# Six experts resident ahead of each pass, gate refills first, and norm statistics by four column groups

## The chip, the cores and the metric

One Trainium2 chip, of which the kernel uses one core. The metric is the device time of one execution in microseconds (us), lower is better. TensorE is PE in the profile (PEld is its weight load), VectorE is DVE, ScalarE is ACT, GpSimd is POOL, and SyncE, which here only issues DMAs, is SP.

## The reference

One inference step of a backbone with two layers over 384 tokens of width 1024: 128 context tokens and 256 latent tokens, all in float32. Layer 0 mixes tokens by attention, layer 1 by window means. Then both layers do the same mixture of experts:

```python
def modulate(x, g, shift, scale):
    return rms_norm(x, g) * (1.0 + scale) + shift
...
        x = x + g1 * m
        h = modulate(x, norm_ffn_g[l], sh2, sc2)
        x = x + g2 * hierarchical_moe(h, moe_w_group[l], moe_w_expert[l], moe_w_gate[l],
                                      moe_w_up[l], moe_w_down[l])
```

`hierarchical_moe` takes for each token the best of 4 groups and in it the best 2 of 8 experts. Each of the 32 experts has a gate and an up matrix of 1024x256 and a down matrix of 256x1024 (`silu(x Wg) * (x Wu)`, times the token's weight, times `Wd`). The shifts, scales and gates of the modulation are one product of the conditioning vector with 1024x6144 weights (`ada_w`) in each layer.

## The kernel before

**Order of the work.** Every engine has its own program, written out by hand; semaphores alone order them. The kernel goes through: loads and products of `ada_w` beside the attention of layer 0 (24 chunks of 2 MB, `ada(i)` on TensorE, L1212); the residual (`x_new`); the norm ahead of the experts (`norm_act`, `norm_dve`, `norm_pe`); the router; the pass over 32 expert tiles of 64 tokens (`experts`, `step`), with an extra tile where an expert has more than 64 tokens; the sum of the results (`total`); the pooling mixer of layer 1; then norm, router, pass and sum again.

**Weights in the pass.** An expert has 2 MB of gate and up weights (`moe_w_in`) and 1 MB of down weights (`moe_w_out`). `ring` holds four experts (`RING`), a fifth lies in `more_gu` (half of `adaw`) and `more_down` (a third of `hT`, and half of `adas`). These five are loaded ahead of the pass. SP then issues the other 27 in one queue (`load_tile`): for expert s it waits until the gate product of the expert that held the place is done, issues the 2 MB (L370), waits for its down product, issues the 1 MB (L374), and only then comes to expert s+1. After the fourth refill of layer 0 it issues `bands` and `poolw`, which the mixer of layer 1 needs. The extra tile's weights (`load_extra`) come last, once the down product of expert 28 is done.

**A step on TensorE.** Gate and up products of expert s (L1523, 32 records), the transposes of the rows of expert s+1 (L1499), the down product of expert s-1 (L1547), the transpose of the hidden values (L1532). In steps 1 to 5 six `keep` jobs stand behind it: four transposes (L1466) that bring the residual x from `xT` back to rows by token, which ScalarE copies into `xtok` (L756). GpSimd gathers the rows of each expert by indirect DMA (L531 the first four, L503 the rest) and scatters the results (L513).

**Norm.** x lies as `xT`, features on the partitions: 8 chunks of 128x384. ScalarE squares chunk k into one of two buffers (L688); TensorE adds it up over partitions with a 128x128 matrix of ones (L1403), so every partition gets the sums of all 384 tokens; ScalarE may square chunk k+2 only after that. Then VectorE scales the sums and adds the epsilon (L948), ScalarE takes the root (L690, in layer 0 with a load of its function table), VectorE the reciprocal of 128x384 (L950), and multiplies `xT` by it chunk by chunk (L951, L954).

**Router.** Logits (L1418), a copy, transposes, then a long row of small VectorE operations that picks the experts; counts (L1442, L1445); the rows of h by token (`rows_by_token`, L1433, copied by ScalarE and stored to DRAM); the numbers over 64 (L1453, L1455); places and one table of indices (L1471), from which the gathers start; a second table (L1478); rows of expert 0 (L1499), their copy (L1073), and the first gate product. In layer 0 `ada(21)` and `ada(22)` stand ahead of the logits, `ada(23)` ahead of `rows_by_token(0)`, and VectorE does six operations (`scales` and two more) of layer 1's modulation between the second table and L1073.

## Time and profile before

| | |
|---|---|
| time, median of 3 runs | 889.2 us (885.93 to 895.58) |
| profiled execution, its own time | 891.41 us |
| profiled execution, span | 889.4 us |
| TensorE busy | 725.8 us (82%) |
| VectorE, ScalarE, GpSimd busy | 355.5, 141.0, 175.1 us |
| moved by DMA | 294.32 MB |
| read from and written to HBM, over the span | 354 GB/s |
| mean granted TensorE clock | 0.937 of full speed |

The span runs from the first to the last instruction of the profiled execution. A granted clock of 1.00 is TensorE's upper level, 0.50 its lower one. A busy TensorE may wait inside of it: ends of matmuls are modelled. DMA share is the mean busy share of the core's 16 DMA engines.

### The profile page before, as it was taken

The page shows a single profiled execution, that of the slowest core. Times are in us where ns is not written, and L with a number is a line of the kernel's source. Part 1 is how long each engine was busy: PE and PEld are TensorE (multiplying, and loading weights), DVE is VectorE, ACT ScalarE, POOL GpSimd, SP SyncE. Part 2 cuts the span into 40 slices and gives each one's busy share as a digit, 9 for nine tenths or more (in the row PEclk, how much of TensorE's full clock was granted, in tenths as well). Part 3 has the DMA queues.
Part 4 walks back from the last instruction along what each step waited for, and adds up shares of the span by engine and source line. Part 5 has one row for each costly group of instructions (what it writes and reads, how often), then busy time and mean ns, then how long its engine had stood idle before and what let it go on. Part 6 is the DMA issues. An engine that isn't in the chain of part 4 may idle for free.

```text
span 889.4 us, 12795 instructions
## 1 busy us (share of the span) xinstructions
PE 725.8 (82%) x4544; PEld 404.3 (45%) x4544; DVE 355.5 (40%) x830; ACT 141.0 (16%) x340; POOL 175.1 (20%) x275
## 2 busy tenths in 40 slices
PE   4899989999968999787778872955999978777870
PEld 3333434468636555444444432624655534444430
DVE  2212457742364444323332334465334433333243
ACT  3111154530250110000000012442110000000000
POOL 0000400000002233333223120002133333322220
PEclk9999999999986999999999996985999999999995
DMA  9999849842793799999999947932699999999925
GB/s 343 428 433 405 216 167 410 304 173 102 324 349 103 305 410 418 422 421 421 421 420 422 389 183 291 425 139 88 242 408 376 422 422 421 421 423 422 417 117 213
DMA packets 39237, 294.32 MB, mean 331 GB/s; under 512 B 10568, under 2 KB 12032, under 8 KB 19232
## 3 DMA queue, kind: packets, MB, share of 16 engines
q1 hardware_dynamic: 26512, 275.51, 75.8%
q0 software_dynamic: 10880, 13.26, 5.0%
q10 hardware_dynamic: 1808, 5.06, 1.4%
q8 instruction: 23, 0.38, 0.2%
q14 instruction: 14, 0.11, 0.0%
HBM read 293.24 MB, written 22.02 MB: 354 GB/s over the span
## 4 chain that ended last, share of the span: by engine, by line
PE 53%; DMA 30%; DVE 7%; issue 6%; SPq 2%; ACT 1%; POOL 0%; POOLq 0%; DVEq 0%
DMA ring<-in_moe_w_in 22%; PE bank L1523 15%; PE bank L1287 7%; PE bank L1547 7%; PE bank L1212 4%; PE bank L1386 3%; DMA ring<-in_ada_w 3%; PE bank L1499 2%; DMA ring<-in_moe_w_out 2%; DMA adaw<-results 2%; PE bank L1394 2%; PE bank L1418 2%; PE bank L1346 1%; PE bank L1327 1%; PE bank L1403 1%
## 5 line engine op out<-in xcount | busy, mean ns | idle before, releaser
L1523 PE MATMUL bank<-ring,qkv 128*64 128x256 f32 x2016 | 241.5, 393 | 63.4 <-issue 39.6
L1523 PEld LDWEIGHTS bank<-ring,qkv 128*64 128x64 f32 x2016 | 157.0, 141 | 130.0 <-issue 66.1
L1073 DVE COPY qkv<-bank 128x512 f32<-128x512 f32 x64 | 44.3, 692 | 220.6 <-PE bank L1499 192.6
L513 POOL DMA_INDIRECT results<-adaw,scur x65 | 67.6, 1040 | 311.6 <-DVE adaw L1096 279.3
L1547 PE MATMUL bank<-ring,qkv 128*64 128x512 f32 x504 | 122.0, 604 | 1.2 <-DVE qkv L1085 0.8
L765 ACT ACTIVATE qkv<-bank 128x128 f32<-128x128 f32 x64 | 17.7, 277 | 452.2 <-PE bank L1523 411.8
L503 POOL DMA_INDIRECT adaw<-rows,gcur x57 | 59.1, 1036 | 44.3 <-POOL gcur L500 35.0
L1287 PE MATMUL bank<-ring,hT 128*128 128x512 f32 x144 | 65.2, 609 | 1.3 <-DVE hT L841 1.3
L1547 PEld LDWEIGHTS bank<-ring,qkv 128*64 128x64 f32 x504 | 31.0, 136 | 47.5 <-issue 45.6
L1085 DVE COPY qkv<-bank 128x128 f32<-128x128 f32 x64 | 18.7, 291 | 76.7 <-PE bank L1532 76.7
L1094 DVE SCALAR_TENSOR_TENSOR adaw<-qkv,wcur 128x512 f32<-128x512 f32 x64 | 48.1, 752 | 2.3
L1096 DVE SCALAR_TENSOR_TENSOR adaw<-bank,wcur,adaw 128x512 f32<-128x512 f32 x64 | 48.1, 751 | 2.3
L1499 PE MATMUL bank<-con,adaw 128*128 128x128 f32 x260 | 43.5, 291 | 2.0 <-DVE adaw L1096 2.0
L1287 PEld LDWEIGHTS bank<-ring,hT 128*128 128x128 f32 x144 | 27.4, 194 | 37.8 <-issue 36.5
L1499 PEld LDWEIGHTS bank<-con,adaw 128*128 128x128 f32 x260 | 28.0, 144 | 26.8 <-issue 26.7
L491 POOL MEMSET adaw<- 128x2048 f32 x2 | 3.6, 1805 | 179.5 <-PE bank L1212 146.3
L1532 PEld LDWEIGHTS bank<-con,qkv 128*128 128x128 f32 x64 | 9.0, 140 | 52.7 <-DVE qkv L1079 51.1
L644 ACT ACTIVATE ring<-bank,ss 128x384 f32<-128x384 f32 (+1 forms) x48 | 24.0, 505 | 36.5 <-DVE ss L899 36.5
L1386 PE MATMUL bank<-hT,ring 128*128 128x256 f32 x128 | 29.1, 380 | 0.0
L1212 PE MATMUL bank<-adaw,condT 128*32 128x512 f32 x240 | 28.9, 598 | 0.0
L1386 PEld LDWEIGHTS bank<-hT,ring 128*128 128x128 f32 x128 | 23.7, 190 | 3.7 <-DVE xT L930 0.8
L1532 PE MATMUL bank<-con,qkv 128*128 128x128 f32 x64 | 21.1, 330 | 2.0 <-DVE qkv L1079 2.0
(227 smaller groups left out, 707.9 us busy)
## 6 DMA issues: line engine op xcount, KB each, us to landing
ring<-in_moe_w_in SPq DMA_DIRECT2D x63, 2048.0 KB
ring<-in_moe_w_out SPq DMA_DIRECT2D x63, 1024.0 KB
adaw<-in_ada_w SPq DMA_DIRECT2D x15, 2048.0 KB, 10.7
ring<-in_ada_w SPq DMA_DIRECT2D x9, 2048.0 KB, 10.6
ring<-in_attn_w_qkv SPq DMA_DIRECT2D x3, 2048.0 KB, 35.5
ring<-in_attn_w_o SPq DMA_DIRECT2D x1, 4096.0 KB, 21.4
adaw<-in_moe_w_in SPq DMA_DIRECT2D x2, 2048.0 KB, 23.9
adaw<-results SPq DMA_DIRECT2D x8, 512.0 KB, 6.1
```

Source lines behind the costliest of these rows:

```text
L503: pool.indirect_dma_start(xg[:, b], None, rows, bass.IndirectOffsetOnAxis(ap=gcur[:, b:b + 1], axis=0), bounds_check=row_limit, oob_is_err ...
L513: pool.indirect_dma_start(res, bass.IndirectOffsetOnAxis(ap=scur[:, p, :], axis=0), yout[:, p], None, bounds_check=res_limit, oob_is_err=F ...
L1073: V.tensor_copy(xgT[:, p], bank[2][:, :]).then_inc(xgT_ready, 1)
L1094: V.scalar_tensor_tensor(yout[:, p], gdiff, wcur[:, p, 1:2], glat, ALU.mult, ALU.add).then_inc(y_order, 1)
L1096: V.scalar_tensor_tensor(yout[:, p], bank[4 + p % 2][:, :], wcur[:, p, 0:1], yout[:, p], ALU.mult, ALU.mult)\
L1212: last = T.matmul(out[32 * j:32 * j + 32, :], condT[:, k, c:c + 32], w[:, k], start=i == SETS[n] and half == 0, stop=i + 1 == SETS[n + 1] ...
L1287: last = T.matmul(bank[5 + g % 3][:, :], hT[:, k, t * P:(t + 1) * P], wqkv[n][:, k, :], start=k == 0, stop=k == KD - 1)
L1386: last = T.matmul(bank[WO_BANKS[d % 2]][:, 0:NTOK - CTX], wo[:, k, d * P:(d + 1) * P], hT[:, k, CTX:NTOK], start=k == 0, stop=k == KD - 1)
L1499: last = T.transpose(bank[2][:, i * P:(i + 1) * P], xg[:, q, i * P:(i + 1) * P], ident)
L1523: last = T.matmul(bank[p][64 * a:64 * a + 64, 0:2 * P], xk[:, k % 4, k // 4], w[:, :, k, a * P:(a + 1) * P], start=k == 0, stop=k == KD - ...
L1532: T.transpose(bank[3][:, 0:P], hid[:, p], ident).then_inc(hid_mm, 1)
L1547: last = T.matmul(bank[4 + p][64 * a:64 * a + 64, :], hidT[:, p, 64 * j:64 * j + 64], w[j][:, a * 512:(a + 1) * 512], start=j == 0, stop=j ...
```

## The change

- **Sixth expert.** A place for expert 5 (`RING + 1`): 1.5 MB of its gate and up weights in `xT`, 0.5 MB in the other half of `adas`, the down weights in two thirds of `hT`. SP issues the first two once all `keep` jobs have read `xT`, the last once the rows of expert 0 are transposed. 26 experts are left to refill. So that `xT` can be split, the gate and up weights are laid out chunk by chunk (gate, up, gate, up) instead of all gate, then all up.
- **Gate refills first.** SP issues the 2 MB of expert s and behind it the 1 MB of expert s-1.
- **`bands` and `poolw`** leave the pass: `bands` is loaded in the router of layer 0, `poolw` behind the results of layer 0. For this the rows by token are written to `qkv` (`rows_out`) and not to `xtok`.
- **`keep` jobs** leave the steps: four stand ahead of the first table (L1471), two ahead of the second (L1478).
- **Norm.** All eight chunks are squared into buffers of their own. TensorE adds them up with 32 columns of ones, chunk k into column group k mod 4. ScalarE copies the sums, three one-column matmuls turn them to tokens on partitions, ScalarE and VectorE make root and reciprocal on 128x3, VectorE multiplies them into three identities (128x384), and one matmul with ones spreads the factors over all partitions. VectorE reads them from PSUM.
- **`ada` chunks.** `ada(21)` and `ada(22)` come behind the transposes of the logits, `ada(23)` behind `rows_by_token(5)`; what waits for them (the load of expert 3 among it) moves along.
- **`scales`** of layer 1 move behind the pass of layer 0.

```diff
-        sq = free[:, 3200:3200 + 2 * NTOK].rearrange("p (b n) -> p b n", b=2)
-        rstd = free[:, 3200 + 2 * NTOK:3200 + 3 * NTOK]
-
+        sq = free[:, 0:KD * NTOK].rearrange("p (k n) -> p k n", k=KD)
+        sums = free[:, 3200:3200 + NTOK]
+
...
+        IN_X = KD * NTOK // (2 * FE)
+        sixth_gu = [xT[:, :, :].rearrange("p k t -> p (k t)"), adas[:, 2:4, :].rearrange("p a n -> p (a n)")]
+        sixth_down = flat_h[:, 0:2 * D]
...
-        s_more, s_more_out = sem("s_more"), sem("s_more_out")
-        LAST = [NE - RING + (b + 1) % RING for b in range(RING)]
-        PER_LAYER = [2 + (LAST[b] - RING - 1 - b) // RING for b in range(RING)]
+        s_more, s_more_out, s_six, s_six_out = map(sem, ("s_more", "s_more_out", "s_six", "s_six_out"))
+        AHEAD = RING + 2
+        LAST = [NE - RING + (b + 2) % RING for b in range(RING)]
+        PER_LAYER = [2 + (LAST[b] - AHEAD - b) // RING for b in range(RING)]
+        EXTRA_SLOT = LAST.index(min(LAST))
...
-
-                def load_tile(s, b, old):
-
+                if l == 0:
+                    sp.wait_ge(s_rowsout, 48)
+                    sp.dma_start(bands, bands_in).then_inc(s_bands, 16)
+                    sp.wait_ge(ada_vec, 4)
+                sp.wait_ge(x1_mm, l * 6 + 6)
+                for part, a, b in ((sixth_gu[0], 0, IN_X), (sixth_gu[1], IN_X, KD)):
+                    sp.dma_start(part, moe_w_in[l, RING + 1, :, a * 2 * FE:b * 2 * FE]).then_inc(s_six, 16)
+                sp.wait_ge(xg_mm, l * NE + 1)
+                sp.dma_start(sixth_down, moe_w_out[l, RING + 1]).then_inc(s_six_out, 16)
+
...
+                def refill_in(s, b, old):
                     sp.wait_ge(gu_mm, s + (l * NE + 1 - old))
                     load_in(l, s, b, s_win[b])
+
+                def refill_out(s, b, old):
                     sp.wait_ge(down_mm, s + (l * NE + 1 - old))
                     load_out(l, s, b, s_wout[b])
...
-                for s in range(RING + 1, 2 * RING + 1):
-                    load_tile(s, s - RING - 1, RING + 1)
-                if l == 0:
-
-                    sp.wait_ge(tab_mm, 2)
-                    sp.dma_start(bands, bands_in).then_inc(s_pool, 16)
-                    sp.dma_start(poolw, pool_w[0].rearrange("g (k p) n -> p g k n", p=P)).then_inc(s_pool, 16)
-                loops = (NE - 2 * RING - 1) // RING
+                def refill(s, b):
+
+                    refill_in(s, b, RING)
+                    refill_out(s - 1, (b - 1) % RING, RING)
+
+                for b in range(RING):
+                    refill_in(AHEAD + b, b, AHEAD)
+                    if b:
+                        refill_out(AHEAD + b - 1, b - 1, AHEAD)
+                refill_in(AHEAD + RING, 0, RING)
+                refill_out(AHEAD + RING - 1, RING - 1, AHEAD)
+                first = AHEAD + RING + 1
...
                     for b in range(RING):
-                        load_tile(r * RING + (2 * RING + 1 + b), b, RING)
-                for s in range(2 * RING + 1 + RING * loops, NE):
-                    load_tile(s, (s - 1) % RING, RING)
+                        refill(r * RING + (first + b), (b + 1) % RING)
+                for s in range(first + RING * loops, NE):
+                    refill(s, (s - 2) % RING)
+                refill_out(NE - 1, (NE - 3) % RING, RING)
...
+                if l == 0:
+                    sp.dma_start(poolw, pool_w[0].rearrange("g (k p) n -> p g k n", p=P)).then_inc(s_pool, 16)
...
-                    if i >= 2:
-                        act.wait_ge(st_mm, m * KD + i - 1)
-                    A.activation(sq[:, i % 2], xT[:, k, :], ACT.Square).then_inc(sq_ready, 1)
-                act.wait_ge(ms_ready, m + 1)
-                A.activation(rstd, rstd, ACT.Sqrt).then_inc(std_ready, 1)
+                    A.activation(sq[:, i], xT[:, k, :], ACT.Square).then_inc(sq_ready, 1)
+                act.wait_ge(st_mm, m * 3 + 1)
+                A.activation(sums, bank[STAT_BANKS[m]][:, 0:NTOK], ACT.Copy).then_inc(std_ready, 1)
+                act.wait_ge(st_mm, m * 3 + 2)
+                A.activation(ss[:, 8:11], bank[STAT_BANKS[m]][:, NTOK:NTOK + TT], ACT.Sqrt, scale=1.0 / (32 * D), bias=C("eps"))\
+                    .then_inc(std_ready, 1)
...
-                    act.wait_ge(s_rowsout, l * 48 + 48)
-                    A.activation(xtok[:, t, q * 512:(q + 1) * 512], bank[6 + n % 2][:, :], ACT.Copy).then_inc(x1_copied, 1)
+                    A.activation(xtok[:, t, q * 512:(q + 1) * 512], bank[4 + n % 2][:, :], ACT.Copy).then_inc(x1_copied, 1)
...
+                for n in range(6):
+                    keep(n)
...
-                    for n in KEEP_AT[s]:
-                        keep(n)
...
-                dve.wait_ge(st_mm, m * KD + KD)
-                V.tensor_scalar(rstd, bank[STAT_BANKS[m]][:, 0:NTOK], 1.0 / D, EPS, ALU.mult, ALU.add).then_inc(ms_ready, 1)
-                dve.wait_ge(std_ready, m + 1)
-                order(V.reciprocal(rstd, rstd))
+                dve.wait_ge(std_ready, m * 2 + 2)
+                order(V.reciprocal(ss[:, 12:15], ss[:, 8:11]))
+                V.tensor_tensor(dg[:, :, :], ident.unsqueeze(1).to_broadcast([P, TT, P]),
+                                ss[:, 12:15].unsqueeze(2).to_broadcast([P, TT, P]), ALU.mult).then_inc(root_ready, 1)
+                rstd = bank[STAT_BANKS[m]][:, 0:NTOK]
+                dve.wait_ge(st_mm, m * 3 + 3)
                 V.tensor_tensor(hT[:, 0, :], xT[:, 0, :], rstd, ALU.mult).then_inc(xr_ready, 1)
...
-                if l == 0:
-                    scales(1, 1, 8)
-                    scales(1, 4, 24)
-                    m = mods[:, 1, 2 * KD:3 * KD, :]
-                    order(V.tensor_tensor(m, m, gains[:, 32:40].unsqueeze(2).to_broadcast([P, KD, 2]), ALU.mult))
-                    order(V.tensor_scalar(constant[:, :, :], mods[:, 1, 0:KD, :], C("column_sum"), None, ALU.mult))
-                    V.memset(ss[:, 18:19], 0.0).then_inc(mods_ready, 1)
...
+            scales(1, 1, 8)
+            scales(1, 4, 24)
+            m = mods[:, 1, 2 * KD:3 * KD, :]
+            order(V.tensor_tensor(m, m, gains[:, 32:40].unsqueeze(2).to_broadcast([P, KD, 2]), ALU.mult))
+            order(V.tensor_scalar(constant[:, :, :], mods[:, 1, 0:KD, :], C("column_sum"), None, ALU.mult))
+            V.memset(ss[:, 18:19], 0.0).then_inc(mods_ready, 1)
             total(0, TILES_BACK[0])
...
                 for k in range(KD):
-                    pe.wait_ge(sq_ready, n // 2 * KD + k + 1)
-                    T.matmul(bank[STAT_BANKS[n // 2]][:, 0:NTOK], ones, sq[:, k % 2], start=k == 0, stop=k == KD - 1).then_inc(st_mm, 1)
+                    pe.wait_ge(sq_ready, m * KD + k + 1)
+                    j = 32 * (k % 4)
+                    last = T.matmul(stat[j:j + 32, 0:NTOK], ones[:, 0:32], sq[:, k], start=k < 4, stop=k >= 4,
+                                    skip_group_check=True)
+                last.then_inc(st_mm, 1)
+                pe.wait_ge(std_ready, m * 2 + 1)
+                for t in range(TT):
+                    last = T.matmul(stat[:, NTOK + t:NTOK + t + 1], sums[:, t * P:(t + 1) * P], ones[:, 0:1],
+                                    start=True, stop=True)
+                last.then_inc(st_mm, 1)
+                pe.wait_ge(root_ready, m + 1)
+                T.matmul(stat[:, 0:NTOK], ones, dg[:, :, :].rearrange("p t n -> p (t n)"),
+                         start=True, stop=True).then_inc(st_mm, 1)
 
...
                 norm_pe(2 * l)
                 if l == 0:
                     pe.wait_ge(x_new[0], KD)
                     vectors(2)
-                    ada(21)
-                    ada(22)
...
                 if l == 0:
-                    ada(23)
+                    ada(21)
+                    ada(22)
...
                 rows_by_token(4)
                 rows_by_token(5)
+                if l == 0:
+                    ada(23)
...
                     if n < 2:
-                        pe.wait_ge(gates_read, l + 1)
+                        pe.wait_ge(hb_copied, l * 6 + 6)
                     else:
                         pe.wait_ge(x1_copied, l * 6 + n - 1)
...
 
+                for n in range(4):
+                    keep(n)
...
+                keep(4)
+                keep(5)
                 pe.wait_ge(slots_ready, l * 12 + 12)
```

## Rows read from the trace of the kernel before

**Rows 1.** Windows: busy us (count) of PE, PEld, DVE, ACT, POOL; clock, DMA share, GB/s.
```profile
354.00:510.00 156.00, 125.08 (x877) 70.72 (x876) 54.60 (x118) 5.27 (x19) 45.68 (x74) 0.99 1.00 417
583.00:619.00 36.00, 22.21 (x95) 14.38 (x95) 21.55 (x85) 13.53 (x19) 4.27 (x4) 0.64 0.25 81
700.00:845.00 145.00, 117.55 (x810) 63.55 (x808) 49.60 (x109) 4.99 (x18) 44.41 (x72) 0.98 1.01 421
```

**Rows 2.** Timeline of SP's queue: start, duration, what; refills of layer 0.
```profile
283.89 0.33 SPq L370 DMA_DIRECT2D ring<-in_moe_w_in  x1
294.19 0.33 SPq L374 DMA_DIRECT2D ring<-in_moe_w_out  x1
...
376.07 0.33 SPq L374 DMA_DIRECT2D ring<-in_moe_w_out  x1
...
497.54 0.33 SPq L374 DMA_DIRECT2D ring<-in_moe_w_out  x1
```

**Rows 3.** Windows of 5 us behind the first refill of either pass.
```profile
289.00:294.00 5.00, 5.00 (x36) 2.82 (x32) 1.58 (x3) 0.28 (x1) 0.00 (x0) 1.00 0.31 134
630.00:635.00 5.00, 5.00 (x38) 3.00 (x34) 1.76 (x4) 0.28 (x1) 0.00 (x0) 1.00 0.36 151
```

**Rows 4.** Timeline of TensorE, layer 0, an expert before its weights are late.
```profile
328.56 3.67 PE L1523 MATMUL bank<-ring,qkv 128*64 128x256 f32 x32
...
334.88 3.67 PE L1523 MATMUL bank<-ring,qkv 128*64 128x256 f32 x32
```

**Rows 5.** Chain that ended last: start, duration, what; extra tile of layer 0.
```profile
508.31 18.27 DMA ring<-in_moe_w_out
```

**Rows 6.** DMA issues: count, KB each, us to landing; two loads of layer 0.
```profile
hT<-in_pool_w SPq DMA_DIRECT2D x1, 1024.0 KB, 15.2
qkv<-in_bands SPq DMA_DIRECT2D x1, 800.0 KB, 12.3
```

**Rows 7.** Timeline of TensorE, last expert of layer 1: gate and up, then down.
```profile
854.19 3.67 PE L1523 MATMUL bank<-ring,qkv 128*64 128x256 f32 x32 [0.90 <-issue]
...
860.22 1.94 PE L1547 MATMUL bank<-ring,qkv 128*64 128x512 f32 x8 [0.38 <-DVE qkv L1085]
```

**Rows 8.** Lines of either norm: duration min/median/max in ns, first and last start.
```profile
L688 ACT ACTIVATE qkv<-xT x16: 522/523/524, 221.1 to 576.9; 128x384 f32<-128x384 f32 x16
L934 DVE SCALAR_TENSOR_TENSOR xT<-bank,mods,xT x8: 350/351/351, 220.7 to 233.2; 128x128 f32<-128x128 f32 x8
L941 DVE SCALAR_TENSOR_TENSOR xT<-bank,mods,xT x16: 350/412/476, 563.4 to 572.6; 128x128 f32<-128x128 f32 x8, 128x256 f32<-128x256 f32 x8
L950 DVE RECIPROCAL qkv<-qkv x2: 2553/2554/2554, 240.4 to 579.6; 128x384 f32<-128x384 f32 x2
L951 DVE TENSOR_TENSOR hT<-xT,qkv x2: 557/558/559, 243.0 to 582.2; 128x384 f32<-128x384 f32 x2
```

**Rows 9.** Timeline of ScalarE, norm of layer 0.
```profile
238.26 1.28 ACT L690 ACT_TABLE_LOAD   x1
```

**Rows 10.** Timeline of TensorE and VectorE, router of layer 0.
```profile
244.41 5.80 PE L1418 MATMUL bank<-hT,wr 128*36 128x384 f32 x16 [0.83 <-DVE hT L956]
251.09 1.92 PE L1212 MATMUL bank<-adaw,condT 128*32 128x512 f32 x16
...
256.75 1.52 PE L1442 MATMUL bank<-rt,con 128*128 128x32 f32 x12 [0.45 <-DVE rt L988]
...
258.49 1.97 PE L1433 MATMUL bank<-con,hT 128*128 128x128 f32 x8
...
272.80 2.79 PE L1478 MATMUL bank<-hT 128*128 128x43 f32 x12 [0.77 <-DVE hT L1040]
...
277.29 0.69 DVE L1073 COPY qkv<-bank 128x512 f32<-128x512 f32 x1
```

**Rows 11.** Timeline of TensorE and GpSimd, router of layer 1.
```profile
583.60 8.30 PE L1418 MATMUL bank<-hT,wr 128*36 128x384 f32 x16 [5.20 <-DVE hT L956]
...
613.81 1.14 POOL L531 DMA_INDIRECT adaw<-rows,gidx  x1 [39.61 <-DVE gidx L1037]
```

More of the change, by code:

```diff
@@ L1571, in _ @@
                 gate_rows()
[L1572 removed]
+                first = AHEAD + 1
+                pe.wait_ge(x1_copied, l * 6 + 6)
                 for s in range(1, first):
                     step(s, s % NBUF, old=s - 1)
[L1575 to L1576 removed]
                 loops = (NE - 1 - first) // RING
```

69 lines of the change are left out of this document (37 added, 32 removed).

## The prediction

> **What bounds the kernel now.** I read the windows first, cut at the stages. In both passes, once the resident experts are used up, the DMA share is 1.00 and 1.01 at 417 and 421 GB/s, while TensorE is busy for only 80% [rows 1]. Then SP's queue: its issues of down weights are 121.47 us apart over 15 experts, 8.10 us each [rows 2]. TensorE alone needs 6.32 us a step, from one gate product to the next [rows 4]. So a pass is a DMA stream: it begins with the first refill and ends with the last one, and TensorE has 1.8 us to spare in every expert. The router of layer 1, the third window, is the opposite: DMA share 0.25, clock 0.64 of full speed, a chain of small steps that hop from engine to engine [rows 1]. What is taken off the stream or off this chain shortens the kernel, microsecond for microsecond; what is moved into the idle queue of the router costs nothing, if it is done before the refills begin.
>
> **The sixth expert.** It takes 3 MB (3.146e6 bytes) off each stream, 7.5 us at 421 GB/s [rows 1], so 15.0 us in both. The pace of 8.10 us contains the rows' own gathers and scatters, which stay; it is the upper bound of the saving, 16.2 us. The 3 MB must be read ahead of the pass instead. In layer 1 DMA engines idle for most of 36 us [rows 1]. In layer 0 the loads between the transposes of the logits and the first refill are expert 3 and the fifth expert (3 MB each), `bands` and the sixth: 9.8 MB, 10.3e6 bytes, or 24 us; from 251 us, where `ada(22)` will now end [rows 10], they are through at 275 if they could be issued back to back. The sixth can't: its gate weights wait for the last `keep`, near 274, and land 5 us later, its down weights near 282. The first refill is due at 283.89 [rows 2]. So they fit, with some 2 us to spare; if the cover fails, the refills start later by what is left over, 2.5 us for the down weights.
>
> **`bands` and `poolw`.** 800 and 1024 KB leave the stream of layer 0 [rows 6]: 1.87e6 bytes, 4.4 us. `bands` goes where the queue of layer 0 is idle, `poolw` behind the results of layer 0, ahead of the loads of layer 1's experts. Those delay nothing, since they wait for a router that is 36 us long; `poolw` itself must land before the pooling products some 20 us later. I cost both at nothing.
>
> **Gate refills first.** After the first refill (2 MB, 5.0 us) SP waits for the down product and the queue runs dry: the next issue comes 10.3 us after the first [rows 2], and the windows behind the first refill show a DMA share of 0.31 and 0.36 [rows 3]. The dry stretch is 10.3 - 5.0 = 5.3 us. In the new order the second gate refill waits only for the gate product of expert 1, which ends 2.6 us before the down product of expert 0 behind it (0.66 + 1.94 us of work on TensorE by the same step). So 2.6 us are won in each layer, 5.2 us; bounds are 0 (another wait ends last) and 5.3 us each. Later in the pass the order changes no rate. At its end it does: the last 3 MB are now 2 MB of gates, then twice 1 MB. Before, the last gate weights land at 854.19 and the down weights 2.5 us later, near 856.7, but the last down product starts only at 860.22 [rows 7], 3.5 us behind its weights, because the whole gate product stands before it. From the landing of the gates to the last down product it is 6.0 us. Now the gates come 5 us before the end, so it starts 1.0 us behind its weights. That gives 2.5 us in layer 1. In layer 0 it gives nothing: there the extra tile follows, its weights are issued at 508.31 and land 18.27 us later [rows 5], right as TensorE asks for them; they stand last in the queue and move with it.
>
> **The norm.** From the last x to the first product with the factors layer 0 takes 243.0 - 233.55 = 9.4 us, layer 1 582.2 - 573.0 = 9.2 us [rows 8]. The new chain: a square 0.52; the last column-group matmul to its reader 1.0 (what the old last matmul took to reach VectorE, I take the same); a copy of 128x384 on ScalarE 0.52; three one-column matmuls 0.45; a root of 128x3 0.2; a reciprocal 0.17 (these three are small and estimated, no row stands for them); the product into `dg` 0.56, as any product of 128x384; the spreading matmul 1.0; six hand-overs of 0.05. That is 4.7 us, against a reciprocal of 2.55 us alone before [rows 8]. In layer 0 the root's function table, 1.28 us [rows 9], now stands between copy and root, with only 0.45 us of matmuls to hide it: 5.5 us. So layer 1 wins 4.4 us, layer 0 3.9 us. No row shows a one-column matmul on `sums` or column groups of 384; from half to twice the chain of 4.7 us, the gain lies between 6.8 and -0.2 us each.
>
> **The router of layer 0 gives it back.** `ada(21)` and `ada(22)` lay under the norm and cost nothing. Now two chunks, 3.84 us, stand where one of 1.92 us stood [rows 10], and the counts behind them had waited only 0.45 us for VectorE: 1.92 - 0.45 = 1.5 us later. `ada(23)` now stands between the last rows and the numbers over 64, on which VectorE waits: 1.9 us at full clock, 3.8 at half. The two `keep` jobs ahead of the second table cost what eight transposes cost in the row of that router at half clock, 1.97 us, less the 0.77 us for which TensorE waited there [rows 10]: 1.2 us. But `scales`, which held the copy of expert 0's rows back for 0.6 us, are gone. Sum: -3.9 + 1.5 + 1.9 + 1.2 - 0.6 = +0.1 us. The other four `keep` jobs lie in 6 us of waiting for VectorE; moved out of the steps they shorten TensorE, which does not bound. `scales` behind the pass lie under the wait for the results.
>
> **The first gather of layer 1** is issued at 613.81 [rows 11], and 2 MB of the sixth expert's gates start about 1 us later. It can be held up by nothing, or by the whole load, 5.0 us. Of its 1.1 us of generation most is over by then, so I take 1.0 us. The Trainium skill, page "DMA: Bandwidth & Descriptors", section "Queues, rings and completion order", says that each DMA engine takes packets from the queue rows in turn. By that rule the gather would not wait for the load's end but alternate with it, near the low end of the range; no row here shows a gather beside such a load alone.
>
> **The sum.** Layer 0: -7.5 - 4.4 - 2.6 + 0.1 = -14.4 us. Layer 1: -7.5 - 2.6 - 2.5 - 4.4 + 1.0 = -16.0 us. Together -30.4: the span of 889.4 becomes 859.0, the profiled execution's own 891.4 becomes 861.0. It was 2.2 us above the median of the three runs, 889.2, so the median to come is 858.8 us.
>
> **Rivals.** (a) The clock falls. The logits of layer 0 took 5.80 us after 0.83 us of waiting, those of layer 1 8.30 us after 5.20 us of waiting [rows 10, 11]: the lower level costs 2.5 us. The new norm takes most of TensorE's work out of its chain, and in layer 0 the two `ada` chunks that filled the gap are gone. If the clock is at its lower level from there on, logits cost 2.5 us more, three `ada` chunks 5.8, eight transposes 1.0: +9.3, so 868 us. The Trainium skill, page "TensorE: Matmul & The Clock Gate", section "Why this matters for your kernels", advises against idle gaps between bursts of matmuls because the clock then drops; by that rule the four column groups speak against the change, and this rival is what it would do. Against it: vectors and the spreading matmul fall into the gap, which is then under 3 us at a time, shorter than the 5.20 us of layer 1. (b) The same, the other way: in layer 1 the gap of 5.20 us is broken up and the clock stays: logits 2.5 us sooner, transposes and tables (2 x 2.8 us at half clock) up to 2.8: 854 us. (c) The change does not do what it says in one part: the sixth loads and the gather get in each other's way, up to 4 us more in layer 1, and late down weights, 2.5 us in each layer: 868 us. (d) TensorE becomes the bound, and the kernel slower than before. In the new layout a gate product reads its 256 columns from two places 1 KB apart instead of 8 KB. If that costs each of the 32 records of a step more than 0.06 us on 3.67/32 = 0.115 us, a step passes 8.1 us and both passes are TensorE's. A pass now takes some 243 us from first gate to last down product (27 x 8.10, 4.4 for the two other loads, 5.3 dry, the rest for its first gate product and its tail). At 0.08 us a record a step is 8.9 us, 32 steps 284 us: twice 41 us lost, 3.5 won outside the passes, 967 us. The point from which it is slower than before is 243 / 32 = 7.6 us a step, 0.04 us a record. Nothing speaks for it: the same engine reads both halves in one pattern today. Without such a price TensorE would come to the last gate product of layer 0 at 328.6 + 24 x 6.32 = 480 us, while the gate weights land near 500 (508.31 + 18.27, less 7.5 for the extra tile, 5.0 for the down weights behind them and the 14.4 us of the sum): it can't bind.
>
> **How the numbers follow.** Forecast 855 to 864, 858.8 likeliest: 0.58. (a) 0.16, (b) 0.10, (c) 0.10, (d) 0.02, and 0.04 for what is between, a stream that saves less than its bytes. The range holds 8 of 10: below it takes in (b) with the pace of 8.1 us (-1.2), 852; above, (a) and (c) at 868 with the upper part of the gap's bound, 870. A measurement of this kernel can tell about 1% from no change. All cases but (d) and part of the rest lie more than 9 us below 889: faster 0.96, same 0.02, slower 0.02.
>
> **What would show it.** Right: DMA share still 1.0 to within some 10 us of each pass's end; SP's down issues still 8.1 us apart; the second refill some 7.7 us after the first instead of 10.3; TensorE's gate product at 6.3 us a step when not late; first product with the factors 5 us behind the last x; the first gate product of layer 0 near 278, of layer 1 some 18 us earlier than now, near 601. Wrong: a pace above 8.1 us, a DMA window below 0.9 in the middle of a pass, clock 0.5 at the logits of layer 0, or rows of expert 0 that wait for their gather.

## The result and the profile after

The changed kernel takes 882.1 us, the median of 4 runs (881.69 to 882.61), against 888.95 us of the kernel before beside it. The ratio is 0.989, with a 95% interval of 0.985 to 0.993. So it is faster by some 7 us, not by the 30 us of the forecast, and outside the range of 852 to 870 us. The profiled execution has a span of 880.3 us, 9.1 us less than the one of before.

I read its trace in the order of the forecast. First the windows, one in the middle of each pass and one over the router of layer 1:

```profile
354.00:500.00 146.00, 125.46 (x877) 66.99 (x871) 54.06 (x116) 5.56 (x20) 48.34 (x78) 0.99 1.01 421
700.00:835.00 135.00, 117.65 (x787) 61.08 (x785) 48.25 (x104) 5.00 (x18) 43.36 (x70) 0.95 1.01 422
581.00:617.00 36.00, 24.45 (x117) 17.97 (x114) 18.79 (x77) 14.55 (x21) 4.54 (x5) 0.69 0.52 186
```

The middle of a pass is the stream that it was [rows 1]: DMA share 1.01, 421 GB/s. In the router's window the share went from 0.25 to 0.52: there the sixth expert's gates are read, and the loads of the other residents, now behind `poolw`, end later than before (a share of 0.65 from 581 to 587, against 0.30 before). The next view is TensorE's timeline where no weights are late:

```profile
325.93 3.67 PE L1572 MATMUL bank<-ring,qkv 128*64 128x256 f32 x32
...
332.25 3.67 PE L1572 MATMUL bank<-ring,qkv 128*64 128x256 f32 x32
```

A step still has 6.32 us and a gate product 3.67 us [rows 4]; the new weight layout costs nothing. The norm's lines follow (duration min/median/max in ns, first and last start in us):

```profile
L712 ACT ACTIVATE qkv<-xT x16: 524/524/526, 220.9 to 572.5; 128x384 f32<-128x384 f32 x16
L714 ACT ACTIVATE qkv<-bank x2: 492/492/492, 234.8 to 574.0; 128x384 f32<-128x384 f32 x2
L716 ACT ACTIVATE ss<-bank,con x2: 264/264/264, 236.6 to 575.4; 128x3 f32<-128x3 f32 x2
L976 DVE RECIPROCAL ss<-ss x2: 176/176/176, 236.9 to 575.7; 128x3 f32<-128x3 f32 x2
L977 DVE TENSOR_TENSOR dg<-con,ss x2: 557/557/557, 237.1 to 575.9; 128x384 f32<-128x384 f32 x2
L981 DVE TENSOR_TENSOR hT<-xT,bank x2: 554/554/555, 239.4 to 577.5; 128x384 f32<-128x384 f32 x2
```

The last x of layer 0 ends at 233.29, so its first product with the factors (L981) comes 6.1 us later; in layer 1 it is 5.0 us. Before it was 9.4 and 9.0 us [rows 8]. The forecast had 5.5 and 4.7 us. The reciprocal of 2.55 us has become one of 0.18 us. Up to here all is as forecast. What is not stands in the chain that ended last (start, duration, what):

```profile
259.92 12.90 DMA rows<-qkv
...
273.77 8.52 DMA adaw<-rows,gidx
...
501.28 22.03 DMA ring<-in_moe_w_out
...
607.79 7.31 DMA adaw<-rows,gidx
```

The first gather of expert rows takes 8.5 us in layer 0 and 7.3 us in layer 1, and the pass waits for both. Rows of expert 0 that wait for their gather were on the forecast's list of what would show it wrong. The first gate product comes at 284.36 in layer 0 (278.03 before; the forecast was near 278) and at 617.18 in layer 1 (619.13 before; the forecast was near 601). Then SP's queue and the windows beside it:

```profile
310.68 0.33 SPq L376 DMA_DIRECT2D ring<-in_moe_w_in  x1
313.13 0.33 SPq L380 DMA_DIRECT2D ring<-in_moe_w_out  x1
329.64 0.33 SPq L376 DMA_DIRECT2D ring<-in_moe_w_in  x1
```

```profile
320.00:325.00 5.00, 5.00 (x42) 2.80 (x40) 2.47 (x6) 0.28 (x1) 1.70 (x3) 1.00 0.81 316
325.00:330.00 5.00, 5.00 (x41) 2.78 (x37) 1.90 (x4) 0.26 (x1) 1.91 (x4) 1.00 0.13 39
330.00:335.00 5.00, 5.00 (x37) 2.53 (x37) 2.79 (x6) 0.02 (x1) 1.35 (x3) 1.00 0.92 332
```

Behind the fourth refill SP issues nothing for 16.5 us, and the DMA engines stand still: 0.13 of their share at 325 to 330. (1.00 - 0.81) x 5 + (1.00 - 0.13) x 5 + (1.00 - 0.92) x 5 = 5.7 us of the stream are lost, a second dry stretch that the forecast did not have. Layer 1 has the same gap, from 646.79 to 663.29, and loses 6.7 us by the same sum (shares of 0.97, 0.43, 0.35 and 0.92 from 650 to 670).

### The profile page after: what moved, and what is told of

It reads as the page before. It is cut to its first block, busy times and chain, and to the rows that moved or that the text cites. A ratio compares the mean times of both kernels' runs of the same rounds, so it can differ in the third digit from the quotient of the medians.

```text
span 880.3 us, 12828 instructions
## 1 busy us (share of the span) xinstructions
PE 731.0 (83%) x4560; PEld 404.0 (46%) x4560; DVE 352.0 (40%) x830; ACT 141.5 (16%) x342; POOL 175.7 (20%) x275
## 3 DMA queue, kind: packets, MB, share of 16 engines
q1 hardware_dynamic: 26800, 275.51, 76.9%
q0 software_dynamic: 10880, 13.26, 4.9%
## 4 chain that ended last, share of the span: by engine, by line
PE 54%; DMA 36%; DVE 4%; issue 2%; ACT 2%; SPq 1%; POOL 0%; POOLq 0%; DVEq 0%; ACTq 0%
DMA ring<-in_moe_w_in 25%; PE bank L1572 17%; PE bank L1316 7%; PE bank L1596 6%; PE bank L1241 4%; PE bank L1415 3%; DMA ring<-in_ada_w 3%; DMA ring<-in_moe_w_out 3%; PE bank L1546 2%; DMA adaw<-rows,gidx 2%; DMA adaw<-results 2%; PE bank L1423 2%; PE bank L1458 2%; PE bank L1375 1%; DMA rows<-qkv 1%
## 5 line engine op out<-in xcount | busy, mean ns | idle before, releaser
L1572 PEld LDWEIGHTS bank<-ring,qkv 128*64 128x64 f32 x1952 | 150.3, 144 | 119.9 <-issue 44.0
L1596 PE MATMUL bank<-ring,qkv 128*64 128x512 f32 x488 | 118.1, 604 | 1.1 <-DVE qkv L1108 0.8
L1596 PEld LDWEIGHTS bank<-ring,qkv 128*64 128x64 f32 x488 | 30.0, 136 | 46.0 <-issue 44.1
L1581 PEld LDWEIGHTS bank<-con,qkv 128*128 128x128 f32 x64 | 9.0, 141 | 52.7 <-DVE qkv L1102 51.1
```

The costliest lines, as they stand in the source:

```text
L1572: last = T.matmul(bank[p][64 * a:64 * a + 64, 0:2 * P], xk[:, k % 4, k // 4], w[k // IN_X if b > RING else 0][:, k % IN_X if b > RING else ...
L1581: T.transpose(bank[3][:, 0:P], hid[:, p], ident).then_inc(hid_mm, 1)
L1596: last = T.matmul(bank[4 + p][64 * a:64 * a + 64, :], hidT[:, p, 64 * j:64 * j + 64], w[j][:, a * 512:(a + 1) * 512], start=j == 0, stop=j ...
```

## The experiments

All ratios are to the kernel before, run beside each kernel; brackets are 95% intervals. The table is worked out from the traces: from the end of the last x to the first gate product (the norm and the router), from there to the gate product of layer 0's extra tile and to the last one of layer 1 (the stream), and from the last x of layer 0 to the end of the span. What lies ahead of that last x is the same code in all kernels, and ends anywhere from 230.0 to 238.2 us; so for the traces the last column is a better measure than the span. There is one trace of each kernel. Where kernels have the same code in a stage, their rows still differ: by 1.3 us in router 0 (44.5, 43.3 and 44.6 for the three with the old norm), and by up to 1.8 us in a stream (227.9 and 226.1). Differences in the table that are smaller than this say nothing by themselves.

| kernel | ratio | router 0 | stream 0 | router 1 | stream 1 | from last x of layer 0 |
|---|---|---|---|---|---|---|
| before | 1 | 44.5 | 248.7 | 46.0 | 235.1 | 655.9 |
| norm alone | 0.996 | 44.6 | 248.4 | 41.5 | 234.5 | 650.6 |
| gate refills first alone | 0.995 | 43.3 | 245.9 | 45.8 | 231.4 | 650.1 |
| bands, poolw alone | 0.996 | 44.6 | 244.6 | 45.7 | 235.7 | 656.0 |
| changed | 0.989 | 51.1 | 239.1 | 44.7 | 227.9 | 647.0 |
| changed, sixth's gates in small loads | 0.979 | 48.7 | 238.0 | 42.4 | 227.4 | 640.0 |
| changed without the sixth | 0.981 | 46.9 | 240.7 | 42.2 | 228.3 | 641.9 |
| the same, keep in the steps | 0.991 | 46.3 | 243.6 | 42.2 | 230.6 | 646.0 |
| sixth's gates later | 0.978 | 45.4 | 239.3 | 41.2 | 226.1 | 636.1 |
| six places once | 0.975 | 51.0 | 233.8 | 45.9 | 219.7 | 634.1 |
| both of these | 0.963 | 46.2 | 234.3 | 41.2 | 219.5 | 624.5 |
| both, ada moved | 0.963 | 43.0 | 234.2 | 40.5 | 219.4 | 622.2 |

**Without the sixth expert.** The loads of the sixth are gone, `AHEAD` is 5.

```diff
-        AHEAD = RING + 2
+        AHEAD = RING + 1
...
-                for part, a, b in ((sixth_gu[0], 0, IN_X), (sixth_gu[1], IN_X, KD)):
-                    sp.dma_start(part, moe_w_in[l, RING + 1, :, a * 2 * FE:b * 2 * FE]).then_inc(s_six, 16)
-                sp.wait_ge(xg_mm, l * NE + 1)
-                sp.dma_start(sixth_down, moe_w_out[l, RING + 1]).then_inc(s_six_out, 16)
```

> The changed kernel without the sixth resident expert: its three loads are gone and experts 5, 6, 7, 8 are the first refills, in gate-first order; the norm and everything else stay. Theory A (two losses eat the sixth: the first gather runs beside the sixth's gate load, which costs about 6 us of layer 0 and 5 us of layer 1, and the queue of refills runs dry a second time for 5.7 us a layer, because a ring of four places has nothing free between refill 9 and the gate product of expert 6): 11 us come back, 2 x (7.5 - 5.7) = 3.6 us are lost, so about 874.5 us, 7.5 us faster than the changed kernel, with the first gate product near 278.5 and no second dry stretch of over 2 us. Theory B (only the gather collides, the sixth is otherwise worth its 7.5 us a layer): 882 - 11 + 15 = 886. Theory C (the sixth is worth all of its 15 us, and the norm or the gate-first order gave less than I summed): 897.

Measured: 876.95 us, ratio 0.981 [0.978, 0.985], against 0.989 [0.985, 0.993] with the sixth. So the sixth expert, costed at a gain of 15 us, gained nothing and more likely made the kernel slower: the two intervals just meet, and from the last x the traces have 647.0 us with it and 641.9 without. Theory C is out, and theory A's 874.5 us is nearer than B's 886. The gather is back at 3.85 us. Theory A had the right parts and too large sizes, though: it gave 11 us back in the routers, and the table has 4.2 and 2.5 us; it took 3.6 us from the streams, and the table has 2.0. And SP's queue shows why the sixth gives the stream so little:

```profile
310.93 0.33 SPq L376 DMA_DIRECT2D ring<-in_moe_w_in  x1
313.38 0.33 SPq L380 DMA_DIRECT2D ring<-in_moe_w_out  x1
323.57 0.33 SPq L376 DMA_DIRECT2D ring<-in_moe_w_in  x1
```

The fifth refill goes into place 0 again, so it waits for the gate product of the first refilled expert: here that is expert 5, and the refill is issued 38.5 us after the first gate product (323.57 - 285.08). With the sixth resident it is expert 6, one TensorE step of 6.32 us later, and it is issued after 45.3 us (329.64 - 284.36). A stream 7.5 us shorter starts its long part 6.8 us later. That leaves 0.7 us, and the streams of the table differ by 1.6 and 0.4 us. With five residents the DMA engines have no such dry stretch: their share is 0.97, 1.02, 1.01 and 0.92 in the four windows of 5 us from 310 to 330, and its lowest in layer 1 is 0.82, from 652 to 657.

**The sixth's gate load after the first gather; six places once; both.** Three kernels. In the first, one wait is moved up:

```diff
+                sp.wait_ge(xg_mm, l * NE + 1)
                 for part, a, b in ((sixth_gu[0], 0, IN_X), (sixth_gu[1], IN_X, KD)):
                     sp.dma_start(part, moe_w_in[l, RING + 1, :, a * 2 * FE:b * 2 * FE]).then_inc(s_six, 16)
-                sp.wait_ge(xg_mm, l * NE + 1)
```

In the second, experts 10 and 11 go into the buffers of the fifth and sixth residents, and the waits and places of experts 12 to 31 follow from that:

```diff
-                for b in range(RING):
-                    refill_in(AHEAD + b, b, AHEAD)
-                    if b:
-                        refill_out(AHEAD + b - 1, b - 1, AHEAD)
+                def again_in(s):
+                    b = s - AHEAD if s < 2 * AHEAD else s % RING
+                    if b < RING:
+                        return refill_in(s, b, AHEAD)
+                    sp.wait_ge(gu_mm, s + (l * NE + 1 - AHEAD))
+                    if b == RING:
+                        sp.dma_start(more_gu, moe_w_in[l, s]).then_inc(s_more, 16)
...
+                for s in range(AHEAD, 4 * RING):
+                    again_in(s)
+                    if s > AHEAD:
+                        again_out(s - 1)
```

> The changed kernel, the sixth expert's gate load held back until the rows of the first expert have been transposed, so that it can't run beside the first gather. Theory A: the first gather of each layer lands 5 to 6 us earlier, the first gate product of layer 0 is near 278.5 instead of 284.4, the second dry stretch stays, 871 us. Rival (the gather is not slow because of that load, but because of the bands or of what the gather is itself): gather stays at 7 to 8.5 us, 882. Rival (the load comes too late for the sixth expert's gate product): a wait of TensorE at the step of expert 5, 878 or more.

> The changed kernel, experts 10 and 11 refilled into the buffers of the fifth and sixth residents as soon as these are free, so that there are six places once over and refill s waits for the gate product of expert s - 6 up to s = 15. The gather's collision stays. Theory A (the second dry stretch is the four-place ring's): no dry stretch near 325 or 659, the stream of weights ends 5.7 us earlier in each layer, 871 us. Rival (the dry stretch is covered, as it was with five residents): 882, with the steps that wait for weights merely beginning elsewhere.

> The two last edits together: the sixth's gate load behind the first gather, and its and the fifth's buffers used again for experts 10 and 11. Theory A: the two losses lie in different places and add up, 860 us, first gate product near 278.5, no second dry stretch. Rival (both feed the same end, the landing of the last refills, and one covers the other): 869 to 871, no better than either alone.

Measured: 873.02 us, ratio 0.978 [0.974, 0.982]; 872.52 us, 0.975 [0.971, 0.979]; 859.53 us, 0.963 [0.959, 0.967]. Theory A gave 871, 871 and 860 us. The chain of the first kernel:

```profile
255.70 12.90 DMA rows<-qkv
...
269.55 3.78 DMA adaw<-rows,gidx
```

The gather takes 3.78 us instead of 8.52 us, though `bands` still runs near it: it was the sixth's load. TensorE does not wait for the late load either: it comes to the sixth expert 6.32 us after the fifth, at 311.22, as at a step without a wait. The row ahead of it, the store of the rows, is as slow as it was; that is another matter, below. The third kernel's queue and window, where the changed kernel stood dry:

```profile
311.35 0.33 SPq L457 DMA_DIRECT2D adaw<-in_moe_w_in  x1
313.81 0.33 SPq L380 DMA_DIRECT2D ring<-in_moe_w_out  x1
317.67 0.33 SPq L460 DMA_DIRECT2D xT<-in_moe_w_in  x1
...
320.13 0.33 SPq L469 DMA_DIRECT2D hT<-in_moe_w_out  x1
```

```profile
320.00:325.00 5.00, 5.00 (x43) 3.01 (x43) 2.31 (x5) 0.28 (x1) 1.36 (x3) 1.00 0.99 412
325.00:330.00 5.00, 5.00 (x41) 2.59 (x37) 2.36 (x6) 0.00 (x0) 1.70 (x3) 1.00 1.02 423
```

The refills of experts 10 and 11 (L457, L460) fill the gap. The two losses lie in different columns of the table and add up. The late load takes 5.7 and 3.5 us off the routers of the changed kernel (45.4 and 41.2 instead of 51.1 and 44.7), and 4.8 and 4.7 us off those of the kernel with six places (46.2 and 41.2 instead of 51.0 and 45.9). The six places take 5.3 and 8.2 us off the streams (233.8 and 219.7 instead of 239.1 and 227.9), and 5.0 and 6.6 us where the load is late. In layer 1 the 8.2 us are 1.5 us more than the dry stretch itself, which is no more than streams of the same code differ by.

**The sixth's gates in eight loads of 2 KB a partition.** In the same place as in the changed kernel:

```diff
-                    sp.dma_start(part, moe_w_in[l, RING + 1, :, a * 2 * FE:b * 2 * FE]).then_inc(s_six, 16)
+                    for c in range(b - a):
+                        sp.dma_start(part[:, c * 2 * FE:(c + 1) * 2 * FE],
+                                     moe_w_in[l, RING + 1, :, (a + c) * 2 * FE:(a + c + 1) * 2 * FE]).then_inc(s_six, 16)
```

> The changed kernel, the sixth expert's gate load cut into eight loads of 2 KB a partition instead of two of 12 and 4 KB, in the same place. The first gather beside it took 8.5 us in layer 0, and 3.8 us without it. Theory E (the engines take one packet of each queue in turn, so a gather waits for one packet of the load at each of its own: with small packets it waits less): gather 5 to 6.5 us, first gate product 2 to 3 us earlier after the gather's issue, about 879 us. Rival (the gather stands behind all bytes issued before it, whatever their packets): 8 to 8.5 us again, 882.

Measured: 874.32 us, ratio 0.979 [0.976, 0.983], and in the chain:

```profile
275.06 6.21 DMA adaw<-rows,gidx
...
605.60 4.46 DMA adaw<-rows,gidx
```

6.2 us instead of 8.5, and 4.5 instead of 7.3. The same bytes beside the gather of layer 0 cost half as much when they come in eight small loads (2.4 us over the 3.8 without that load, instead of 4.7). The time is 5 us under the 879 us expected; the table has 2.4 and 2.3 us in the routers, and the rest is of the size by which its rows scatter. The gather's 5 to 6.5 us were expected if the engines take one packet of each queue in turn. The changed kernel's page has 13.26 MB in 10880 packets on the gathers' queue, 1.2 KB each, and 275.51 MB in 26800 on the weights', 10.3 KB each. Turn about, a gather packet of that size would wait for 10 KB of weights, and the gather would last as long as there are weights.

The Trainium skill, page "DMA: Bandwidth & Descriptors", section "Queues, rings and completion order", says that an engine changes between queue rows only at packet boundaries. The trace fits that rule, but it does not single it out, and no run shows that the page's packet is what the profile counts as one.

The rival, a gather that waits for all bytes issued ahead of it, was expected at 8 to 8.5 us. The 6.2 us do not exclude it, because eight issues also take longer than two. In the changed kernel SP had issued all 2 MB at 274.90, and GpSimd's issue of the gather ended at 274.93. Here SP issues the eight loads from 275.28 on, half a microsecond apart, and GpSimd's issue ends at 276.16, so that two or three of the eight stood ahead of the gather. What is shown is that the sixth's gate load makes the gather late, and that eight small loads halve this; whether by turns or by fewer bytes ahead is not.

**The ada blocks moved.** Added to the kernel with both edits: `ada(21)` and `ada(22)` go into TensorE's two pauses in the norm of layer 0, `ada(23)` behind the overflow products.

```diff
+                if n == 0:
+                    ada(21)
                 pe.wait_ge(std_ready, m * 2 + 1)
...
+                if n == 0:
+                    ada(22)
                 pe.wait_ge(root_ready, m + 1)
...
                 last.then_inc(over_mm, 1)
+                if l == 0:
+                    ada(23)
```

> The last kernel (sixth's gate load late, six places once over) with one more edit: of the three blocks of modulation products, two go from behind the logits into the two pauses of TensorE in layer 0's norm, and the third from ahead of the overflow products to behind them. In that kernel VectorE stands idle 2.93 us for the counts and 3.18 us for the overflow products, and the last rows store takes 12.85 us beside the weights of expert 3 and of the fifth, whose loads wait for these blocks. Theory A (these blocks cost about what I gave them, 1.5 and 1.9 us, and their place also makes the rows store late): the first gather is issued 5 us earlier after the logits' start, the norm gets 1.6 us longer, 856 us. Rival (the gather then waits for something else that is as late, or the longer norm eats it): 859 to 860, no change. Rival (the rows store is slow whatever is loaded beside it): store of 12 to 13 us again, 860.

Measured: 860.36 us, ratio 0.963 [0.960, 0.967], the same as without it; an edit worth 3 us is not resolved by these intervals. By the time alone the second rival (no change) is right. The trace shows part of theory A's mechanism in layer 0 all the same: router 0 is 43.0 instead of 46.2 us, and the first gather is issued 29.0 us after the logits' start instead of 32.9, where 5 us less were expected. The third rival, a store that is slow whatever is loaded beside it, is out. Two rows changed. The logits, in the changed kernel first, with TensorE's two pauses ahead of them, and in this one second:

```profile
235.31 0.83 PE L1440 MATMUL bank<-con,qkv 128*128 128x1 f32 x6 [0.58 <-ACT qkv L714]
237.69 1.65 PE L1444 MATMUL bank<-dg,con 128*128 128x384 f32 x2 [1.55 <-DVE dg L977]
...
240.80 7.08 PE L1458 MATMUL bank<-hT,wr 128*36 128x384 f32 x16
```

```profile
244.06 5.78 PE L1484 MATMUL bank<-hT,wr 128*36 128x384 f32 x16 [0.66 <-DVE hT L1008]
```

and the stores of the rows in the list of DMA issues (count, KB each, median us to landing), again the changed kernel first:

```profile
rows<-qkv ACTq DMA_DIRECT2D x3, 512.0 KB, 12.1
```

```profile
rows<-qkv ACTq DMA_DIRECT2D x3, 512.0 KB, 6.4
```

Before, these stores took 4.8 us. They run beside whatever waits for `ada(22)`, the weights of expert 3 and of the fifth. SP issued these 0.8 us ahead of the logits' start before (243.64 against 244.41), 11.7 us behind it in the changed kernel (252.46 against 240.80), and 2.2 us ahead of it here (241.82 against 244.06). VectorE's waits for the counts and for the overflow products are 2.73 and 2.54 us instead of 2.93 and 3.18 us, so of what I had laid on these blocks' own time little was there. The logits of layer 0 took 6.9 to 8.3 us in all seven kernels that have the new norm with empty pauses and the logits right behind it; this is the only one in which they did not.

**The parts alone.** On the kernel before: the new norm; the gate-first order of refills; `bands` behind the stored rows and `poolw` behind the results. Their edits are those of the diff ahead of the prediction, so the last alone is shown:

```diff
-                    sp.wait_ge(tab_mm, 2)
-                    sp.dma_start(bands, bands_in).then_inc(s_pool, 16)
...
+                if l == 0:
+                    sp.wait_ge(s_rowsout, 48)
+                    sp.dma_start(bands, bands_in).then_inc(s_bands, 16)
```

> The kernel before with the new norm alone (statistics by four column groups, factors on 128 x 3, spread by a product with the diagonal matrix). My sum gave this 3.9 us in layer 0 and 4.4 us in layer 1. Theory A (the norm did what was forecast and the loss was elsewhere): 8 us under the kernel before, ratio 0.991. Rival (the shorter norm is given back, by a lower granted clock in the logits that follow, 7.1 us instead of 5.8 us in the changed kernel, or by waits for loads that don't move with it): 4 us or less, ratio 0.996 or more.

> The kernel before with the gate-first order of refills alone, five residents. My sum gave it 2.6 us in each layer for the first dry stretch and 2.5 us in the tail of layer 1, 7.7 us. Theory A: 7 us under the kernel before, ratio 0.992. Rival (the order only moves the wait: the gate weights come sooner and the down weights of the expert ahead later, so the end of the stream stays where it was): ratio 0.998 to 1.0.

> The kernel before with one edit: bands goes behind the fifth expert's loads, after the rows are stored, and poolw behind the results of layer 0, instead of both behind the first four refills. My sum gave this 4.4 us, for 1.87e6 bytes less in the stream of layer 0: 4 us under the kernel before, ratio 0.995, the whole of it between the first and the last gate product of layer 0. Rival (bands now lies beside the rows' own traffic and makes the first gather late, or poolw is late for the pooling products): ratio 0.998 to 1.002.

Measured: 888.33 us, ratio 0.996 [0.993, 0.998]; 887.48 us, 0.995 [0.993, 0.998]; 889.07 us, 0.996 [0.995, 0.998]. By the table `bands` and `poolw` gave 4.1 us of stream 0, the order 2.8 us of stream 0 and 3.7 us of stream 1. The order's 0.995 lies between its theory (0.992) and its rival (0.998 to 1.0). Of the 4.1 us of `bands` and `poolw` nothing is left in that trace from the last x to the end (656.0 against 655.9 us): the extra tile's gate product, right behind stream 0, took 6.18 us instead of 3.67, and the piece from its start to the last x of layer 1 is 3.3 us longer. The medians have 3.9 us all the same. The norm gave 4.5 us of router 1 and nothing of router 0. There the norm is 3.3 us shorter, but this kernel leaves `ada(21)` and `ada(22)` where they hid under the old one:

```profile
240.39 1.65 PE L1420 MATMUL bank<-dg,con 128*128 128x384 f32 x2 [1.55 <-DVE dg L952]
241.83 1.74 PE L1228 MATMUL bank<-con,adas 128*128 128x22 f32 x8
243.50 3.54 PE L1217 MATMUL bank<-adaw,condT 128*32 128x512 f32 x16
246.87 1.89 PE L1217 MATMUL bank<-ring,condT 128*32 128x512 f32 x16
248.69 5.35 PE L1436 MATMUL bank<-hT,wr 128*36 128x384 f32 x16
```

They stand 5.2 us between the norm and the logits. The rival of that expectation has the right size (3.3 us less by the medians, 5.3 by the traces). Its reason, a lower clock, is there, but not in the logits: `ada(21)` took 3.54 us here and 1.92 before. The larger part is that the two blocks no longer lie under the norm, which it does not name.

**The keep jobs back in the steps.** On the kernel without the sixth:

```diff
-                for n in range(4):
-                    keep(n)
...
                 for s in range(1, first):
                     step(s, s % NBUF, old=s - 1)
+                    for n in KEEP_AT.get(s, ()):
+                        keep(n)
```

> The changed kernel without the sixth expert (as in the second kernel tried) and with the six jobs that turn x back to tokens put back into TensorE's steps of experts 1 to 5, where the kernel before has them. Its stream of layer 1 took 235.5 us from first to last gate product before, 233.4 us with the gate-first order alone, 228.3 us without the sixth; I had costed these jobs at nothing, since TensorE does not bound. Theory D (they do bound at the start of a pass, where each refill waits for a product and the steps last 6.76 instead of 6.32 us): 233 us again in layer 1, some 4 us more in each layer, 883 to 886 us. Rival (the router gets shorter by what its TensorE is spared, and the stream loses nothing): the time without the sixth, 877, or a little less.

Measured: 884.52 us, ratio 0.991 [0.988, 0.994] against 0.981 [0.978, 0.985]; theory D. The streams are 2.9 and 2.3 us longer. TensorE's timeline, this kernel first, without the jobs second:

```profile
306.49 0.60 PE L1504 MATMUL bank<-con,xT 128*128 128x128 f32 x4
307.02 3.67 PE L1563 MATMUL bank<-ring,qkv 128*64 128x256 f32 x32
...
313.25 0.60 PE L1504 MATMUL bank<-con,xT 128*128 128x128 f32 x4
313.78 3.67 PE L1563 MATMUL bank<-adaw,qkv 128*64 128x256 f32 x32
```

```profile
307.21 3.67 PE L1568 MATMUL bank<-ring,qkv 128*64 128x256 f32 x32
...
313.53 3.67 PE L1568 MATMUL bank<-adaw,qkv 128*64 128x256 f32 x32
```

A step of 6.76 us against one of 6.32 us. Theory D had 4 us more in each layer, so its size was too large. The medians differ by 7.6 us, the traces by 4.1 us (646.0 and 641.9); the intervals allow both, and I take the traces' figure.

## Why the prediction was wrong

**The sixth expert: the step that failed.** "It takes 3 MB off each stream, 7.5 us" is right about bytes, and I let the stream begin where it began. I had written that a pass is a stream from the first refill to the last; it has a gap in between that the number of places sets. Four refills are 12.6e6 bytes, 30 us at 421 GB/s; the fifth must wait for the product of an expert that is itself a refill, and each resident beyond the ring's four puts that product one step of 6.32 us later. With five residents the gap was filled. With six it is the dry stretch: 5.7 and 6.7 us by its windows, 5.3 us of stream 0 and 8.2 us of stream 1 by the kernel that mends it. The rows for it were in the trace of before: a step of 6.32 us [rows 4], the first refill 5.9 us after the first gate product [rows 2], and the rule of places in the code. I used them only for the first gap.

**The gather: the term that was mis-sized.** I took 1.0 us for layer 1 and nothing for layer 0, within a bound of 5.0 us. It was 4.7 us by the gather's own rows in layer 0 (8.52 - 3.78), and by the table's routers with and without the late load 5.7 and 4.8 us in layer 0, 3.5 and 4.7 us in layer 1, so near the upper bound. Rival (c) named the collision and put it at 0.10, and only in layer 1. I had drawn the low end from turns between queues. If turns are the mechanism, which is not shown, they count in packets, and the other side's are eight times as long; so the rule gave no reason for the low end.

**The router of layer 0.** Forecast: +0.1 us. Without the gather's loss it is +0.9 to +2.4 us (45.4 and 46.2, and 46.9 without the sixth, against 44.5). The norm gave 3.3 us where I had 3.9. Two things ate it: the logits, 7.08 us instead of 5.80 us at a granted clock of 0.76 of full speed from 241 to 248, which is rival (a) in one place only, and the slow stores of the rows, since I moved `ada(22)` without following the loads that wait for it. With TensorE's pauses filled by the `ada` blocks the logits ran at 1.00 again. Rival (b) is not shown. The logits of layer 1 took 6.98 instead of 8.30 us, but two kernels with the old norm and the same wait of 5.20 us had 6.80 and 6.79 us there: behind one and the same wait these logits vary by 1.5 us from kernel to kernel.

**The router of layer 1.** 4.4 us were forecast for the norm; the norm alone gave 4.5 us by the table and 4.1 by its own rows (from the last x to the first product with the factors, 9.1 and 5.0 us).

**`bands` and `poolw`, the order of refills.** 4.4 us forecast, 4.1 measured. For the order 2.6 forecast and 2.8 measured in layer 0, 5.1 forecast and 3.7 measured in layer 1; the tail gave less than its 2.5 us.

**The keep jobs.** "Moved out of the steps they shorten TensorE, which does not bound" was wrong too, in the other direction: 2.9 and 2.3 us, a term that stood at nothing. TensorE does not bound the pass, but its first steps release the first refills.

**The sum.** From the last x of layer 0 on, the trace is 8.9 us shorter (655.9 and 647.0), where 30.4 were forecast. Stream 0 is 4.9 us short of its forecast (9.6 of 14.5), stream 1 5.4 us (7.2 of 12.6), router 0 6.5 us (+6.6 instead of +0.1), router 1 2.1 us (1.3 of 3.4), and 2.7 us lie in the extra tile of layer 0 and what stands between it and the last x of layer 1.

The stream terms without the failed step, at the sizes that the kernels with one part showed: layer 0 had 17.3 us to win (7.5 + 4.1 + 2.8 + 2.9) and won 9.6; layer 1 had 13.5 (7.5 + 3.7 + 2.3) and won 7.2. Mending the ring alone won 5.3 and 8.2 us more, which is 2.4 us short of that sum in layer 0 and 1.9 us over it in layer 1; with the gather mended as well the kernel is at 0.963 [0.959, 0.967] of the kernel before, 32.2 us less by the medians side by side (859.53 and 891.73). That this lies near the forecast's 30.4 us is in part luck: 5.2 us of it are the keep jobs, which the forecast had at nothing, and they make up for the order's tail and the router of layer 0. The extra tile of layer 0 took 2.1 us more as well, which no term of the forecast had: its gate product lasted 5.72 us instead of 3.67, after a wait of 2.68 us for its weights, in a window of clock 0.71 (523 to 531). In every kernel of the table but the kernel before and the norm alone it lasted 5.2 to 6.6 us; those two had the clock at 1.00 there. Why the piece from its start to the last x of layer 1 differs by up to 3.3 us between kernels (46.4 to 49.7 us) stays open beyond that.

## What to carry to other kernels

Buffers that hold something once are not places of a ring: count for each refill which product frees its place, and put that time beside the time at which the queue has worked off what it holds. A prefetch into an "idle" queue is not free if a small transfer on the critical path runs there; issue it behind that transfer, or cut it small. And when an engine does not bound a stage, look at whether it still releases the first transfers of that stage.

## What the runs showed of the hardware

- A gather of 1.2 KB packets took 3.8 us in layer 0 without the sixth expert's gate load beside it, 8.5 us beside that load of 2 MB in two pieces with rows of 12 and 4 KB, and 6.2 us beside the same bytes in eight pieces with rows of 2 KB.
- Stores of 512 KB took 4.8 us before and 12 to 13 us in the changed kernel, beside 6 MB of weight loads issued up to 8 us ahead of them; with 5 of these 6 MB issued 11 us ahead of the first store instead of 2 us, 6.4 us. In layer 1, where the same stores have few loads beside them, it was 2.6 us.
- Sixteen matmuls of the logits took 7.08 us at a granted clock of 0.76, after pauses of 0.58 and 1.55 us in the norm, and 5.78 us at 1.00 with these pauses filled. The same held for all seven kernels with these pauses empty and the logits right behind (6.9 to 8.3 us). That pauses so short are enough was not expected.
- Matmuls into column groups of 32 with 384 columns: the profile's sixteen records in 1.90 us in layer 0, against 6.22 us for the sixteen records of the full ones that they replace.
